# A hybrid decoder layer with grouped experts: rows over 128 in tiles of 32 instead of 64, with two reordered places ahead of them

## The reference, cut to what matters

```python
h = x + concat([swa_attention(...), mlstm(...)]) @ w_out
t = rms_norm(h)
# router: best of 4 groups, then the best 2 of its 4 experts; 2 weights for each row
for e in range(16):
    y += combine[:, e:e+1] * ((silu(t @ w_gate[e]) * (t @ w_up[e])) @ w_down[e])
out = h + y
```

## Time and profile before

| | us |
|---|---|
| median of 3 runs | 911.85 (910.15 to 912.02) |
| the profiled execution, its own time | 920.25 |
| its span | 918.4 |
| mean granted TensorE clock | 0.979 of full speed |

### The profile page before, as it was taken

The page is one execution under the profiler, slowest core; times in us unless marked ns, Lnnn a source line. Parts: engine busy times, 40 slices in busy tenths (PEclk is TensorE's granted clock), DMA queues, the critical chain, the costliest instruction groups (busy, mean ns, idle before and its releaser), DMA issues. The chain is left out here.

```text
span 918.4 us, 18022 instructions
## 1 busy us (share of the span) xinstructions
PE 869.4 (95%) x5316; PEld 689.9 (75%) x5317; DVE 615.3 (67%) x1260; ACT 568.0 (62%) x1011; POOL 248.7 (27%) x388
## 2 busy tenths in 40 slices
PE   6999999999999979899977999999999999999994
PEld 4888888888888866688866776776777787677873
DVE  3866666676666667445577856672769599776991
ACT  3765574737465566222140876694788799787980
POOL 4101101010201100100041254544353544355451
PEclk9999999999999999999977999999999999999997
DMA  9701010100001062445391887776597999879972
GB/s 328 259 25 46 1 47 0 46 23 23 23 23 64 8 181 75 163 152 183 128 331 30 322 314 223 244 282 201 208 365 287 337 392 390 275 273 340 392 262 47
DMA packets 54448, 167.92 MB, mean 183 GB/s; under 512 B 9488, under 2 KB 11856, under 8 KB 54416
## 3 DMA queue, kind: packets, MB, share of 16 engines
q1 hardware_dynamic: 47312, 143.12, 42.2%
q0 software_dynamic: 7088, 24.39, 10.2%
q10 hardware_dynamic: 16, 0.01, 0.0%
HBM read 142.96 MB, written 24.54 MB: 182 GB/s over the span
## 5 line engine op out<-in xcount | busy, mean ns | idle before, releaser
L1091 PE MATMUL bank_j<-w_high,rows_high 128*128 128x512 f32 x512 | 206.4, 403 | 0.0
L1093 PE MATMUL bank_j<-w_high,rows_low 128*128 128x512 f32 x512 | 200.5, 392 | 0.2 <-issue 0.2
L1092 PE MATMUL bank_j<-w_low,rows_high 128*128 128x512 f32 x512 | 200.4, 391 | 0.0
L607 POOL TENSOR_TENSOR tick<-mhalf 1x1 f32<-1x1 f32 x171 | 89.1, 527 | 192.5 <-DVE lg L2206 67.3
L1091 PEld LDWEIGHTS bank_j<-w_high,rows_high 128*128 128x128 f32 x512 | 96.5, 189 | 29.9 <-issue 9.1
L2094 DVE TENSOR_TENSOR w_low<-w_res,w_high 128x1024 fp32r<-128x1024 f32 x96 | 114.2, 1218 | 7.0 <-ACT w_high L713 7.0
L1093 PEld LDWEIGHTS bank_j<-w_high,rows_low 128*128 128x128 f32 x512 | 96.5, 189 | 21.3 <-issue 0.6
L1092 PEld LDWEIGHTS bank_j<-w_low,rows_high 128*128 128x128 f32 x512 | 96.7, 189 | 18.3 <-issue 0.2
L713 ACT ACTIVATE w_high<-w_res 128x1024 fp32r<-128x1024 f32 x96 | 97.5, 1050 | 0.0
L1157 PE MATMUL bank_j<-hnT,w_res 128*128 128x128 f32 x512 | 60.3, 276 | 0.0
L1157 PEld LDWEIGHTS bank_j<-hnT,w_res 128*128 128x128 f32 x512 | 58.4, 192 | 0.9
(11 more groups left out here) (393 smaller groups left out, 1835.7 us busy)
## 6 DMA issues: line engine op xcount, KB each, us to landing
w_res<-in_w_gate_dram SPq DMA_DIRECT2D x48, 512.0 KB, 3.9
w_res<-in_w_up_dram SPq DMA_DIRECT2D x48, 512.0 KB, 7.3
bias<-in_w_down_dram SPq DMA_DIRECT2D x32, 512.0 KB
slot_b<-in_w_gate_dram SPq DMA_DIRECT2D x16, 512.0 KB
PT<-in_w_up_dram SPq DMA_DIRECT2D x16, 512.0 KB
gmix<-in_w_down_dram SPq DMA_DIRECT2D x16, 512.0 KB
h<-in_w_down_dram SPq DMA_DIRECT2D x16, 512.0 KB
hn<-in_x_dram SPq DMA_DIRECT2D x8, 512.0 KB, 3.4
```

The lines of the kernel that those rows point to most:

```text
L607: pool.tensor_tensor(tick[:, len(ticks):len(ticks) + 1], mhalf[0:1, 0:1], mhalf[0:1, 0:1], ALU.mult)
L1091: pe.matmul(out_, ah, bh, start=start, stop=False)
L1092: pe.matmul(out_, ah, bl, start=False, stop=False)
L1093: return pe.matmul(out_, al, bh, start=False, stop=stop)
```

## The change

Rows above 128 go in small tiles of 32 rows, each computed in four column quarters of TensorE's array. Gate and up are computed in one part instead of two; results stand in 32 partitions for each 128 hidden columns, and the down product gives 32 partitions for each 256 output columns. `rows_T(t + 1)` comes before the transpose of the tile's own result. The weight of each of the 32 rows is brought to all four groups of partitions by a product with one column (`replicate`) in the middle of the down product. Lists of rows have a column for each 32 rows. Full tiles keep their order. Two other edits: `out_high(1)` moves behind `state_squares`, and the first `keep_busy` goes from 7 to 18.

```diff
-    HP = P // 2
+    QP = P // 4
...
-                        sp.wait_ge(pe_dnp, full * FC + half_order.index(i - 2 * FC) + 1)
+                        sp.wait_ge(pe_dnp, full * FC + i - 2 * FC + 1)
...
                     cp(cin[:, :, TAPS - 1:], ...).then_inc(act_cin, 1)
-                    if into_last:
-                        out_high(1)
                 if main:
                     head_copy(t)
                     state_squares(t, t + 2)
                 if into_last:
-                    for i in range(2, 4):
+                    for i in range(1, 4):
                         out_high(i)
...
-            keep_busy(7)
+            keep_busy(18)
             h2_T(TILES - 1)
...
+            cp(replicate.rearrange("p (q m) -> p q m", q=4),
+               ident[0:QP, 0:QP].unsqueeze(1).to_broadcast([QP, 4, QP]))
             rows_hi(0)
...
# ScalarE
+            def small_tile(t, h):
                 act.activation(warm[:, 0:1], warm[:, 1:2], ACT.Silu)
+                act.wait_ge(pe_gup, (FC + 1) * (t + 2))
+                wait(act, dve_mh, 2 * t)
+                act.activation(sg[:, 0:P], J0[:, 0:P], ACT.Silu).then_inc(act_silu, 2)
+                act.wait_ge(pe_hT, 2 * t + 1)
+                wait(act, pe_dnp, FC * (t + 1))
+                cp(raw_hidden[:, :], S0[:, 0:P]).then_inc(act_hT, 2)
                 rows_hi(t + 1)
                 rows_raw(t + 1)
+                weigh_small(t, h)
...
# TensorE
+            def small_tile(t, e):
                 pe.wait_ge(act_raw, t + 1)
                 wait(pe, dve_mh, 2 * t)
+                for k in range(KC):
+                    j, kk = k // 2, k % 2
+                    if kk == 0:
+                        for i in (k, k + 1):
+                            pe.wait_ge(ld_piece[i], e * 16 + landed[i])
+                    for g in range(1 if j < 3 else 2):
+                        for q in range(4):
+                            at, cols = slice(q * QP, (q + 1) * QP), slice(q * P, (q + 1) * P)
+                            out_ = J0[at, 0:2 * P] if j < 3 else J0[at, g * P:(g + 1) * P]
+                            b = raw_both[j][:, :, kk, cols] if j < 3 else raw_gu[j][g][:, kk, cols]
+                            ins = pe.matmul(out_, raw_rows[:, k, 0:QP], b, start=(k == 0), stop=(k == KC - 1),
+                                            skip_group_check=True)
+                    if kk == 1:
+                        ins.then_inc(pe_gup, 2 if k == 1 else 1)
                 rows_T(t + 1)
+                pe.wait_ge(dve_mh, 2 * t + 1)
+                wait(pe, dve_hT, 2 * t)
+                pe.transpose(S0[:, 0:P], mh[:, 0:P], ident[:, :]).then_inc(pe_hT, 1)
                 wait(pe, y_ready, 2 * t)
+                pe.wait_ge(act_hT, 2 * t + 2)
+                for c in range(FC):
+                    if c == 2:
+                        pe.wait_ge(dve_mh, 2 * t + 2)
+                        pe.matmul(X0[:, 0:1], replicate, wt_t[0:QP, 1:2], start=True, stop=True).then_inc(pe_hT, 1)
+                    pe.wait_ge(ld_piece[2 * FC + c], e * 16 + 32)
+                    for q in range(4):
+                        ins = pe.matmul(S1[q * QP:(q + 1) * QP, 0:2 * P], raw_hidden[:, c * QP:(c + 1) * QP],
+                                        slot[2 * FC + c][:, q * 2 * P:(q + 1) * 2 * P], start=(c == 0), stop=(c == FC - 1),
+                                        skip_group_check=True)
                     ins.then_inc(pe_dnp, 1)
...
# VectorE
-            NH = HT - 2
+            NH = QT - 4
...
-                chain(dve.tensor_copy(lists[:, 0::2, :], rows[:, :, :]))
+                chain(dve.tensor_copy(lists.rearrange("p (a q) w -> p a q w", q=4),
+                                      rows[:, 0:NL // 4, :].unsqueeze(2).to_broadcast([P, NL // 4, 4, 2])))
...
+            def small_tile(t, h):
+                dve.wait_ge(act_silu, 2 * t + 2)
+                wait(dve, pe_hT, 2 * t)
+                dve.tensor_tensor(mh[:, 0:P], sg[:, 0:P], J0[:, P:2 * P], ALU.mult).then_inc(dve_mh, 1)
+                pick_weights(t, 1, dve_mh)
                 dve.wait_ge(act_hT, 2 * t + 2)
                 dve.sem_inc(dve_hT, 2)
                 rows_lo(t + 1)
+                dve.wait_ge(pe_hT, 2 * t + 2)
+                wait(dve, y_ready, 2 * t)
+                dve.tensor_copy(wt_t[:, 2:3], X0[:, 0:1]).then_inc(dve_wt, 1)
                 dve.wait_ge(pe_dnp, FC * (t + 2))
...
```

More of the change, by code:

```diff
@@ L207, in hymba_layer_program @@
         rows = sb("rows", [P, TCOLS, 2])
[L208 to L211, removed]
+        lists = hnT[:, :, :].rearrange("p a b -> p (a b)").rearrange("p (a c) -> p a c", c=2)
+        NL = NE * QT
+        replicate = GT[0:QP, :]
         order_t = sb("tile_order", [P, 1])
-        raw_rows = sb("rows_raw", [P, KC, HP])
-        raw_hidden = darg[:, 1:3, :]
+        raw_rows = sb("rows_raw", [P, KC, 2 * QP])
+        raw_hidden = darg[:, 1, :]
         row_g, row_s, row_h = (sb(n, [P, 1], I32) for n in ("row_g", "row_s", "row_h"))
-        wt_t = sb("wt_t", [P, 2], F32)
+        wt_t = sb("wt_t", [P, 3], F32)
         pieces_of = lambda b, n: [b[:, i * PW:(i + 1) * PW] for i in range(n)]
@@ L535, in _ @@
             with sp.Fori(0, NE - 1) as e:
-                halves = sp.value_load(tabi[0:1, bass.ds(e + LAST, 1)], min_val=0, max_val=MAXT - NE)
-                full = halves + e
+                smalls = sp.value_load(tabi[0:1, bass.ds(e + LAST, 1)], min_val=0, max_val=MAXT - NE)
+                full = smalls + e
                 for i in range(PIECES):
@@ L667, in _, with tile @@
             pool.wait_ge(dve_lists, 4)
-            def tile(t, fulls, halves, landed, listed, rows_out):
+            def tile(t, fulls, smalls, landed, listed, rows_out):
                 pwait(ld_g, 16 * t + 32)
@@ L675, in tile @@
                 pwait(st_full, 16 * fulls)
[L676 removed]
+                pwait(st_small, 16 * smalls)
                 pick(listed, t)
@@ L2132, in _ @@
             one = slice(0, 1)
-            halves = new(NE)
-            chain(dve.scalar_tensor_tensor(halves, cum, -1.0, iota_f[:, 0:NE], ALU.add, ALU.subtract))
-            dve.tensor_copy(tabi[:, LAST:LAST + NE], halves[one, :])
-            dve.scalar_tensor_tensor(tabi[:, FIRST:FIRST + NE], halves[one, :], 1.0, te[one, :], ALU.add,
+            smalls = new(NE)
+            chain(dve.scalar_tensor_tensor(smalls, cum, -1.0, iota_f[:, 0:NE], ALU.add, ALU.subtract))
+            dve.tensor_copy(tabi[:, LAST:LAST + NE], smalls[one, :])
+            dve.scalar_tensor_tensor(tabi[:, FIRST:FIRST + NE], smalls[one, :], 1.0, te[one, :], ALU.add,
                                      ALU.subtract).then_inc(dve_tab, 1)
@@ L2150, in order_of_tiles @@
                 tt(at, t_, n_rows, ALU.subtract)
[L2151 removed]
+                chain(dve.tensor_scalar(at, at, 4.0, None, ALU.add))
                 chain(dve.scalar_tensor_tensor(n_end, n_end, at, at, ALU.mult, ALU.subtract))
[L2153 to L2154 removed]
+                chain(dve.scalar_tensor_tensor(at, n_past, float(QT), n_end, ALU.mult, ALU.subtract))
+                dve.tensor_scalar(order_t[:, :], at, float(NL - 1), None, ALU.min).then_inc(dve_lists, 1)
             order_of_tiles()
             def list_columns():
[L2160 to L2165 removed]
+                chain(dve.tensor_copy(lists.rearrange("p (a q) w -> p a q w", q=4),
+                                      rows[:, 0:NL // 4, :].unsqueeze(2).to_broadcast([P, NL // 4, 4, 2])))
+                own = lists[0:QP, :, :].rearrange("p (e c q) w -> p e c q w", e=NE, q=4)
+                for q in range(1, 4):
+                    part = rows[q * QP:(q + 1) * QP, 0:NL // 4, :].rearrange("p (e c) w -> p e c w", e=NE)
+                    dve.tensor_copy(own[:, :, 1:, q, :], part[:, :, 1:, :]).then_inc(dve_lists, 1)
             def columns():
@@ L2273, in _ @@
             with dve.Fori(0, NE - 1) as e:
-                last = half_tiles(e) + e
+                last = small_tiles(e) + e
                 def split(a, b):
```

136 lines of the change are left out of this document (42 added, 94 removed).

## The result

The kernel after the change takes **905.17 us** (median of 7 runs, 903.16 to 908.3), the kernel before beside it 911.85 (7 runs, 910.0 to 912.13): a ratio of 0.9934, 95% interval 0.9922 to 0.9947. I had forecast 904.0 in a range of 893 to 914. The profiled execution took 903.4 us.

What follows compares the result with a forecast made beforehand. The prediction took TensorE, busy 95% of the span, as the bound. Its terms summed to -7.7 us, set against the profiled 920.25 (giving 912.5) and taken off the median 911.85: 904.0, range 893 to 914.

Steps and rivals of the forecast that it cites:

- Terms 1 and 2: Mixer's end and routing, ahead of the expert loop: moving `out_high(1)` gives -3.5 us, `keep_busy(18)` gives -3.0.
- term 2: Routing of the last row tile: `keep_busy(18)` fills TensorE's idle and keeps the clock up, -3.0 us (bounds 0 and 4.9).
- Rival D: Mixer and routing: DMA landings and the clock take back the gains of both front edits, 910.7 us; 8%.
- Term 3: Lists of rows ahead of the first full tile: VectorE's larger copy costs +0.8 us (0.3 to 1.2).
- Term 4: Experts with one small tile: 8.6 us for a half tile's 12.2, -3.6 each, -18.0 for five.
- Term 5: Pairs of small tiles, experts 1 and 5: second waits for its gather, 17.2 us for 12.2, +10.0 in all.
- Term 6: Expert 4's three small tiles: the third waits for its gather, 25.7 us for 24.8, +0.9 (-0.7 to +4.5).
- Term 7: TensorE's clock falls between gate and up and down in three of twelve small tiles, +5.1 us.
- Rival C: Expert loop: the clock falls in every small tile, twelve falls instead of three, 919.5 us; 9%.
- Rival B: Experts 1, 4, 5: gathers behind additions land at the upper ends, +16.4 and +4.5, 914 us; 11%.
- Rival A: Expert loop: no clock falls, the handovers keep it up, 899 us; 22%.

Runs made afterwards that it cites:

- the first edit alone: `out_high(1)` moved behind the head copy as the only edit to the kernel before: 910.61 us, ratio 0.9985.
- before again: The kernel before, unchanged, run and profiled a second time: 911.86 us, ratio 1.0005.
- the hybrid: Front edits, half tiles kept, and one small tile only where the last 64 rows have 32 or fewer: 905.86 us, ratio 0.9939 to the kernel before.
- the experiment with short additions: The kernel after, with additions of the full tiles of experts 0 to 14 cut to their first 32 rows: 901.56 us, ratio 0.9888 to the kernel before.
- Small tiles alone: The kernel after with `out_high(1)` and the first `keep_busy` put back as before: 908.71 us, ratio 0.9955 to the kernel before.
- the front edits alone: The kernel before with only `out_high(1)` moved and `keep_busy` raised from 7 to 18: 909.48 us, ratio 0.9972.
- the last kernel: The kernel after with two result buffers and every small tile's gather issued ahead of the addition before it: 897.36 us, ratio 0.9838 to the kernel before.
- the buffer alone: The kernel after with two result buffers for small tiles, used in turn: 900.76 us, ratio 0.9885 to the kernel before.
- the order alone: The kernel after with GpSimd's gather for the first small tile issued ahead of the full tile's addition: 920.11 us, ratio 1.0099 to the kernel before.

## Why the prediction was right or wrong, step by step

The forecast of 904.0 met 905.17, and the sign was right. But that the number fitted so well is luck, since two errors cancelled: the front gave 4.5 us less than summed, and the loop of the profiled execution 4.9 more. (The sum itself, 7.7 off 911.85, is 904.15; I had rounded it to 904.0.)

- **Terms 1 and 2** (-3.5 and -3.0) were over-sized: alone they gave 1.0 and 0.7, together 2.0. The mechanisms were mostly as told: head copy near 322 (320.57), `qT` late next, `h2_T` at full clock. The low clock behind the gap before the scores, of which I had counted a part as gained, stayed for 6.8 us with the first edit alone. The step that failed is the sum against the profiled time. I took 8.4 us off for what that execution had above the median, and priced both terms by stalls (5.76, 6.0, low clock under the positions) which owed their size to that same excess; so part of it was counted twice. For term 2 the lower bound, that the clock falls again, was nearer: it falls behind the wait for `sqk`. Rival D, that the clock and landings take the front back, was mostly true of the front itself.
- **Term 3** (+0.8): VectorE's copy took 0.4 more, not 0.8. Expert 0's full tile took 515.02 - 494.81 = 20.2 us for 19.55 before, +0.7, which looks right; but that tile is 19.55 to 20.02 in the five profiles of kernels with half tiles alone (20.02 in before again), and 20.06 to 20.21 in the seven with the new lists. So the term is about +0.3, and the rest of the 0.7 is the first profile's.
- **Term 4** (-3.6 each): -4.1 to -4.2 in the seven profiled kernels that have small tiles alone (-4.5 in the hybrid). Quarters overlap as read from the router: 48 instructions of 256 columns in 2.80 us where 24 in halves took 2.81. Mis-sized was the place of the product: VectorE is done 0.9 us sooner than I took, the own transposes start at +4.9. The one-column product costs 0.30, between its bounds. Five times: -20.9 for -18.0.
- **Term 5** (+10.0): the pairs took 18.8 and 17.8 for 17.2, +12.2 in all. The gather's end, taken at 13.2 behind the first start, was 13.2 and 13.7; the rest, 4.0, took 4.1 at full clock. The number was right and its reason wrong. I bounded the landing by the addition ahead in the queue; the experiment with short additions shows that the pair's gather lands no sooner behind a short one. It is its issue, behind GpSimd's work for the addition, that counts. Missing was the wait for `y_small`, which made the full tiles behind 0.5 and 1.6 us longer: +14.3 with them, within the bounds of 8 to 16.4.
- **Term 6** (+0.9): 24.7 for 24.85 of two half tiles, -0.2. The wait for the third tile's gather, taken to land at 21.7, did not come: GpSimd issued it at 15.4 behind the first start, not 17.1, and it landed at 19.9, before it was needed. The 1.0 us of waiting stood in the second tile instead.
- **Term 7** (+5.1, three falls): one fall in the loop, and its 1.5 us are in the 18.8 above. Small tiles alone had two, of 10 and 7 us.
Rival C took the clock to fall in all twelve. It fell in none of the five singles of the seven profiled kernels with small tiles alone, 35 in all, each 7.96 to 8.10 us long, though 1.4 us of transposes and 0.75 of idle stand between their products. In small tiles it fell only where the wait for the gather came on top.
By the Trainium skill (TensorE: Matmul & The Clock Gate, Part 4: PE-mode transpose) a transpose "doesn't count as PE-busy the same way". These traces go against twelve falls, which is what I had made of it; they do not show how a transpose counts.

In the loop then: -20.9 + 14.3 - 0.2 + 0.7 = -6.1, as 375.7 - 381.8 has it, where the terms had -1.2. With the 2.0 of the front that is 8.1; the runs show 6.7. The executions of the pairs differ (loop lengths of 375.7 and 380.7 with the same tiles), and the medians put less on the loop than this profile: 2.8 us for the small tiles alone, 4.3 for after over the front edits alone.
Rival B (the gather behind the addition) named the right place at too high a price and with the wrong cause. Rival A had the clock nearly right, with one fall for its none, and its 899 was missed all the same, mostly by what the front did not give. That the last kernel comes to 897.4 does not speak for it: rival A kept the waits of the pairs, and there they are gone.

## What to carry to other kernels

Before pricing a stall from one profiled execution that stands above the median, run it again: what is above the median lies somewhere, and it may be in the stall. When tiles shrink, look at what was sized for the old length: here the order of gathers and additions on GpSimd's queue and a single result buffer were hidden by a 12 us tile and bare behind an 8 us one. The two were bound together: the buffer alone gave 4.4 us, the order alone cost 15, and both, at every tile, gave 7.8. And count the loop heads of a dynamic loop as work, on each engine.

## What the runs showed of the hardware that I had not expected

- A loop over tiles that is never entered, with its test and its load from the table, cost 20.8 us over 16 experts by the medians; in the profiles 12.1 in the loop, with ScalarE's idle behind its loop heads at 11.4 + 9.4 us instead of 5.4 + 4.5, and 8.3 ahead of it.
- A gather of 128 rows landed 4.2 to 9.7 us behind its issue in the kernel after (median 7.3). In the pairs it took 4.7 and 5.3, and in expert 1 the same 4.7 behind a 128-row addition, which landed 3.0 us after the gather's issue, and behind a 32-row one, which landed 0.2 after it.
- The clock fell in the second small tile of a pair behind idles of 1.46 + 0.58 us (after, expert 1) and 1.93 + 0.58 (two buffers, expert 5), and stayed up behind 1.96 + 0.58 (after, expert 5) and 1.47 + 0.58 (additions of 32 rows, expert 1). In the singles, with 0.17 + 0.58, it stayed up each time.
